# Attention in a hybrid block: each head's value matmuls are issued behind the probability transposes of the next head

## What is computed

```python
    def one_block(args):
        qi, bi = args
        s = jnp.einsum('bqhd,bkhd->bhqk', qi, k, preferred_element_type=jnp.float32) * scale
        ...
        s = jnp.where(mask[None, None], s, -jnp.inf)
        p = jax.nn.softmax(s, axis=-1).astype(v.dtype)
        return jnp.einsum('bhqk,bkhd->bqhd', p, v)
...
        attn = chunk_causal_attention(q, k, v).reshape(B, T, H * V_HEAD_DIM)
        y_a = jnp.matmul(attn, w_o_mla[l])
        ...
        merged = gates[..., :D] * y_a + gates[..., D:] * y_b
        x = x + jnp.matmul(merged, w_out[l])
        h2 = rms_norm(x, g_ffn[l])
        x = x + hierarchical_moe(h2, ...)
```

## Time and profile before

| | |
|---|---|
| median of 3 runs | 1296.21 us (1293.45, 1296.21, 1296.26) |
| the profiled execution | span 1294.0 us from its first to its last instruction; no device time of it is given apart |
| PE busy | 1216.5 us, 94% of the span |
| PE weight loads busy | 844.8 us, 65% |
| DVE, ACT, POOL busy | 598.3, 302.9, 200.3 us |
| chain of work that ended last | PE 87%, DVE 4%, ACT 3%, POOL 2%, issue 2%, DMA 1% |
| attention stage | from about 361 to 622 us of the span |

### The profile page before, as it was taken

How to read it: one execution, slowest core, us unless ns; L and a number is a source line. 1 busy time by engine, 2 the same in 40 slices (tenths; PEclk the granted TensorE clock), 3 DMA queues, 4 the chain that set the end, 5 groups by cost and what they waited for, 6 DMA issues and landing times.

```text
span 1294.0 us, 14232 instructions
## 1 busy us (share of the span) xinstructions
PE 1216.5 (94%) x5180; PEld 844.8 (65%) x5180; DVE 598.3 (46%) x922; ACT 302.9 (23%) x528; POOL 200.3 (15%) x246
## 2 busy tenths in 40 slices
PE   5999999999978999999999899759999999999996
PEld 5988888886645577776788788744444444444443
DVE  3338999993424454544466334551222222222222
ACT  3432111113433444444222111100101110110110
POOL 3010000000232332120000000021222222222222
PEclk8999999999969999999899999759999999999999
DMA  6011111110100000000420332179999999999991
GB/s 221 1 49 49 49 49 49 49 49 17 41 1 1 1 1 1 1 28 6 163 66 0 102 147 98 66 238 347 317 322 303 295 310 302 329 337 297 300 299 29
DMA packets 138979, 172.25 MB, mean 133 GB/s; under 512 B 12303, under 2 KB 119994, under 8 KB 138938
## 3 DMA queue, kind: packets, MB, share of 16 engines
q1 hardware_dynamic: 127866, 154.86, 36.2%
q0 software_dynamic: 11008, 16.82, 5.4%
q10 hardware_dynamic: 64, 0.02, 0.0%
HBM read 167.45 MB, written 27.26 MB: 150 GB/s over the span
## 4 chain that ended last, share of the span: by engine, by line
PE 87%; DVE 4%; ACT 3%; POOL 2%; issue 2%; DMA 1%; SPq 0%; DVEq 0%; POOLq 0%; ACTq 0%
PE pb L1431 19%; PE pb L1170 12%; PE pb L1171 12%; PE pb L1172 12%; PE pb L1448 10%; PE pb L1310 4%; PE pb L1287 4%; PE pb L1423 3%; PE pb L1299 2%; PE pb L1219 2%; PE pb L1229 1%; PE pb L1370 1%; PE pb L1181 1%; POOL ssh L479 1%; PE pb L1439 1%
## 5 line engine op out<-in xcount | busy, mean ns | idle before, releaser
L1431 PE MATMUL pb<-wgu,hgT 128*128 128x512 f32 x576 | 253.8, 594 | 0.0
L1431 PEld LDWEIGHTS pb<-wgu,hgT 128*128 128x128 f32 x576 | 109.8, 191 | 137.8 <-issue 137.8
L838 DVE SCALAR_TENSOR_TENSOR cv<-up,dwc,cv 128x1024 f32<-128x1024 f32 x120 | 154.1, 1284 | 3.7
L1170 PE MATMUL pb<-hT_hi,ws_hi 128*128 128x512 f32 x384 | 151.7, 395 | 0.0
L1172 PE MATMUL pb<-hT_hi,ws_lo 128*128 128x512 f32 x384 | 149.5, 389 | 0.0
L1171 PE MATMUL pb<-hT_lo,ws_hi 128*128 128x512 f32 x384 | 149.4, 389 | 0.0
L1448 PE MATMUL pb<-wed,midT 128*128 128x512 f32 x288 | 130.2, 595 | 0.0
L771 ACT ACTIVATE yb<-pb,wcol 128x512 f32<-128x512 f32 x36 | 24.7, 687 | 360.3 <-PE pb L1448 360.3
L1154 DVE COPY midT<-pb 128x256 f32<-128x256 f32 x36 | 15.3, 425 | 188.2 <-PE pb L1439 188.2
L1448 PEld LDWEIGHTS pb<-wed,midT 128*128 128x128 f32 x288 | 51.9, 190 | 52.0 <-issue 51.7
L531 POOL DMA_INDIRECT hg<-h_rows,icol x40 | 41.8, 1045 | 264.9 <-DVE icol L1144 244.4
(11 more groups left out here) (268 smaller groups left out, 1795.1 us busy)
## 6 DMA issues: line engine op xcount, KB each, us to landing
wgu<-in_w_e_gate SPq DMA_DIRECT2D x36, 1024.0 KB, 10.9
wgu<-in_w_e_up SPq DMA_DIRECT2D x36, 1024.0 KB, 17.1
wed<-in_w_e_down SPq DMA_DIRECT2D x36, 1024.0 KB, 14.5
ws_raw<-in_w_in SPq DMA_DIRECT2D x24, 512.0 KB, 3.7
xs<-in_x SPq DMA_DIRECT2D x8, 512.0 KB, 9.5
wout<-in_w_out SPq DMA_DIRECT2D x1, 4096.0 KB, 12.7
xb<-in_x SPq DMA_DIRECT2D x8, 512.0 KB, 5.0
h_rows<-h SPq DMA_DIRECT2D x8, 512.0 KB, 2.7
```

Of the source, the lines that this page charges most:

```text
L838: i = v.scalar_tensor_tensor(out=cv[:, c, :], in0=src, scalar=w, in1=cv[:, c, :], op0=ALU.mult, op1=ALU.add)
L1170: t_.matmul(out, w(0), m(0), start=start, stop=False)
L1431: m = t_.matmul(pb[:, GU_BANK[q % 2], :], hgT[q % 2][:, k, :], wgu[q][:, k, :], start=(k == 0), stop=(k == KD - 1))
```

## The change

`pv` of head n no longer stands at the end of step n. It is issued in step n + 1, directly behind `probs_T(n + 1)`; the last one stands behind the loop. No instruction is added or removed, and DVE, ACT, POOL and SP keep their order.

```diff
             for n in range(NTILE * HEADS):
                 j, h = divmod(n, HEADS)
                 probs_T(n)
+                if n:
+                    pv(n - 1)
                 for k, t in slots(j, h, 0):
                     misc(k, t)
                 if n + 2 < NTILE * HEADS:
                     scores(n + 2)
                 for k, t in slots(j, h, 1):
                     misc(k, t)
-                pv(n)
+            pv(NTILE * HEADS - 1)
             misc("oT", NTILE - 1)
```

## The result

The changed kernel takes 1298.62 us (median of 14 runs, 1297.56 to 1299.73) against 1295.68 for the kernel before beside it (14 runs, 1293.45 to 1296.76): ratio 1.0022, interval 1.0014 to 1.0030. It is 2.9 us slower, and the sum had said 0.35 us faster. That is less than the 0.3% that was called no change, and clear of the interval all the same; the time lies 0.3 us above the predicted range.

A forecast was written before the change was run, and what follows sets the result against it. PE was taken to bound the kernel. Terms of +0.18 (exponential), +0.66 (passages) and -1.19 us (end of the attention) sum to -0.35, from 1296.21 to 1295.9 us; range 1291.8 to 1298.3 us.

The forecast's parts named there:

- the waits for the copy: PE's 6.3 us in 6 waits for DVE's copy of transposed probabilities move from value matmuls to transposes, none removed.
- the waits for ACT at the key/value projection: PE's 6.8 us in 6 waits before the second key/value projection stay; 0 won.
- the period of a steady head: In block 7 a head keeps its 4.69 us; another period would speak against the forecast.
- the exponential: Transposes of heads 12 and 20 wait for it: 0.2 us absorbed at 12, +0.18 us kept at 20.
- the passages: Between blocks, DVE's normalisation waits for later value matmuls: +0.66 us in sum, bounds 0 and +1.5.
- hand-offs on PE: Scores directly behind value matmuls cost 0; the other end was 0.27 us per head, 62 times, 16.7 us.
- The other sign: If the forecast is right, the whole attention lasts as long as before within 1 us.
- the gain at the end: Value matmuls of head 62 fill PE's wait for head 63's copy: -1.19 us, bounds -1.2 and -0.6.
- Rival (b): At the attention's end, 32 value matmuls in a row bring the clock back sooner: 3.6 us less, 1292.3 us; chance 0.11.
- Rival (c): Scores' first load waits for value matmuls to end, 0.27 us per head; in full 1312.9 us; chance 0.07.
- (a): The waits for DVE's copy vanish because transposes start sooner: 6.3 us won, 1289.9 us; chance 0.05.
- (d): The exponential is late at every head, not only 12 and 20, needing 2.1 us to vanish; chance 0.03.

The follow-up runs named there:

- only_edges: Against the kernel before, only the pairs at the passages between blocks are swapped; 1297.04 us, one run with no interval.
- tail_only: Against the kernel before, only the last pair swapped (transposes of head 63 ahead of value matmuls of head 62); 1294.45 us against 1295.56, ratio 0.9993.
- early_tail: Against the kernel before, two branch weight tiles (heads 60, 61) moved ahead of row maximum and exponential, last pair alone swapped; 1291.88 us, ratio 0.9972.
- e58_after: Against the kernel before, the two weight tiles moved ahead likewise and to heads 58 and 59, every pair swapped; 1292.37 us, ratio 0.9976.
- e58_tail: Against the kernel before, the two weight tiles moved ahead likewise and to heads 58 and 59, only the last pair swapped; 1289.28 us, ratio 0.9956.
- all_but_tail: Against the kernel before, every pair swapped but the last; 1299.0 us, ratio 1.0025.

## Why the prediction was wrong

What held: the waits for the copy moved to the transposes and did not go (6.4 us for 6.3, in five places and not in the six that were named, since the value matmuls of head 62 fill the last); the waits for ACT at the key/value projection stayed (6.9 for 6.8); the period of a steady head stayed 4.69; the exponential costs 0.19 at head 20 (0.18 forecast) and is absorbed in blocks 0 and 1; the passages are held by the normalisation. They were put at 0.16, 0.3 and 0.2 for the rest, and measured 0.19, 0.39, 0.20 and 0 in only_edges: 0.66 forecast, 0.79 found.

What failed first is the step on hand-offs on PE, "So I take 0 for the new neighbours". They cost 0.05 us where transposes of bank 7 or `oT` stand ahead of the pair, and at a few other heads. From block 3 on the steps of the table add up so: 2.48 - 0.63 = 1.85 us, less 0.79 for the passages, leaves about 1.1 us that the sum did not have. Over all blocks it is 2.34 us, less 0.79 and the exponential's 0.19, so about 1.4 us. The step went from neighbours that the old trace had (transposes behind value matmuls, whose loads start 0.27 us before the value matmuls end) to neighbours that it had not (scores behind value matmuls). The sign that was to show it, another period than 4.69 us in block 7, looked at the one kind of head in which the loss is given back. The other sign, an attention as long as before within 1 us, did fail: it became 2.6 us longer up to the first branch matmul.

The prediction cited a rule of the Trainium skill ("TensorE: Matmul & The Clock Gate", Part 3, on what overlaps and what doesn't): weight loads overlap with matmuls in flight only in other row groups. By the prediction's reading of that rule each of the new neighbours would cost 0.27 us. The traces disagree: the small steps of the table are 0.04 to 0.06 us at some heads and 0 at others. The cause inside PE of the 0.05 stays open: the traces show it, no run explains it.

What failed second is the condition that the text itself set on the gain at the end: "Gain -1.19 us if the clock does the same as now." Its mechanism was right: up to the first branch matmul the swap is worth 1.3 to 1.7 us (tail_only, early_tail, e58_after, e58_tail), and 1.1 where all of it runs at half clock (18.62 against 17.48). With the long wait in place the branch matmuls take half of that back, and 0.7 is left in tail_only; this is the case that the text gave as its bound of -0.6, a half clock that ends when it did before (626.6 us in both traces). But both bounds took the clock to fall as now against PE's work. The blocks' own 2.3 us of delay shifted PE against it, the whole tail ran at 1.2 GHz, and this cost 1.2 us, a term that the sum did not have. The sum with measured terms: +2.34 in the blocks where +0.84 was forecast, and +0.54 behind them (-0.65 for the swap, +1.2 for the delay) where -1.19 was forecast: 2.9 us.

Rival (b), that 32 value matmuls in a row bring the clock back sooner, is refuted: they ran 6.93 us on end at 1.2 GHz in the changed kernel and the clock stayed. Rival (c) was right in kind, a fifth of its size where it shows (0.05 for 0.27 us), and about 1.4 of its 16.7 us in all. Rivals (a) and (d) did not happen. The upper end of the range, 1298.3 us, had no working behind it: neither the +1.5 us of the passages nor any part of the hand-offs went into it. The chance of 0.76 for less than 0.3% covers what was measured (0.22%), but by luck, since the forecast had the sign wrong and the terms it lacked happened to stay under 3.9 us.

## What to carry to other kernels

A swap of two neighbours on the bound engine removes no wait that both of them share; it only moves it. Look at which one an engine behind them is waiting for, and at what each piece costs next to its new neighbours, in every kind of place that the loop has and not in the steady one alone. In this kernel a wait of 2.3 us on PE had a second price, the clock behind it (13.65 to 17.07 us at 1.2 GHz in seven of the nine traces with it, 3.41 to 6.83 in the five without), and that price changed when the work far ahead shifted by two microseconds. So remove the wait first (here a weight tile moved to where DVE and ACT were idle, worth 3.4 us of the medians), then take the order where it pays (the last pair alone, together 5.9 us, ratio 0.9956).

## What the runs showed of the hardware that I had not expected

A group of 8 value loads of 128x128 took 0.84 us with transposes behind it and 0.89 with scores behind it, and 4 transposes 0.45 us behind value matmuls and 0.43 behind other transposes. The granted clock stayed at 0.50 while PE worked 6.93 us without a pause on 64-column matmuls. And the same sequence of groups, 16 value matmuls, 8 transposes, 16 value matmuls with the same waits, took 17.1 to 17.3 us from the mask matmul of head 63 to the first branch matmul in the kernel before and 18.62 in all_but_tail, where PE got there 2.3 to 2.5 us later and the clock fell at nearly the same distance from the start of the attention (249.5 and 249.9 us).
